# Projections two to six of the state-space layer as seven block products instead of eight

## The chip, the cores and the metric

The kernel runs on one core of one Trainium2 chip. The metric is the device time of one execution in microseconds. Three executions of the kernel before took 1654.04, 1657.95 and 1659.07 us, so the median is 1657.95 us. TensorE (PE in the rows, its weight loads PEld), VectorE (DVE), ScalarE (ACT), GpSimd (POOL) and SyncE (SP) each run their own list of instructions in order and wait for one another on semaphores.

## The reference, cut to what matters

Two blocks of two layers each are computed on 256 tokens of width 1024: gated convolutions, stick-breaking attention and two mixtures of experts, then a layer that joins a state-space scan with dilated attention, and a layer of block attention. The change touches only the opening of the state-space layer:

```python
def ssd_dilated_layer(x, norm_w, w_in, conv_w, conv_b, ...):
    h = rms_norm(x, norm_w)
    proj = jnp.einsum("bsd,df->bsf", h, w_in.astype(h.dtype))
    z, xbc, dt, q, k, v, g = split_cols(proj, EVEN_IN_SIZES)
    xbc = jax.nn.silu(causal_dwconv(xbc, conv_w, conv_b))       # 4 taps
    xs, bm, cm = split_cols(xbc, (SSD_D_INNER, ...))
    dt = jax.nn.softplus(dt + dt_bias)
    ...
    cb = jnp.einsum("bclgn,bcsgn->bgcls", Cc, Bc)
    ...
    y = y.reshape(Bsz, S, SSD_D_INNER) * jax.nn.silu(z)
```

All arithmetic is in float32. `xbc` has 2048 channels, `z` has 1024, so these two are 3072 of the columns of `w_in`.

## The kernel before, in words

The weights of a layer come in chunks of 2 MB (1024 x 512 numbers) that SyncE loads into a ring of slots. In the last two layers three slots hold chunks; the other three are free for sums of weights and of inputs. The state-space layer begins with six channel-wise chunks, g to g+5: the first four give `xbc`, the last two `z`. For each, TensorE holds 128 x 128 of the weights and streams all 256 tokens past them (`channels`, L712): 4 blocks of 128 channels x 8 steps over the 1024 inputs are 32 matmuls of 256 columns. Every float32 matmul leaves two records in the trace, so a chunk is 64 records of L719.

What follows a chunk, in the order written out by hand in `ssd_dilated` of each engine:

- ScalarE copies each of the four channel blocks from PSUM into `ss_pad` (L2001) and writes the last tap of the convolution with its bias into `xa` (L2004). After the fourth chunk it loads the table for silu and runs 16 silus (L2009); for chunks five and six it applies silu straight from PSUM into `ss_z` (L2012).
- VectorE adds the three other taps per block (L2814, L2817), each waiting for the one before. Between chunks two and three it computes dt (`steps`, L2795 to L2802).
- TensorE turns the `xs` part into token rows with transposes (`turn_x`, L1472) around chunk six; VectorE scales them into `ss_x` (L2833). Then come four pairs of matmuls B by C (L1492 and L1493), of which the third waits until all four parts of `ss_x` are done, since it writes the PSUM bank that they are read from. Then the scan begins: `run_sum` (L1505) on TensorE, `decay` (L2845, L2847) on VectorE.

Chunks g+6 to g+14 (queries, keys and values) already use seven block products in a layout with tokens on the output's partitions (`seven`, L1312): both operands are cut in halves, four sums of weight blocks (`w_sums`, L2645, one instruction of 128 x 1024 each) and four sums of input blocks (`x_sums`, L2620) are made on VectorE, and seven products of half size in each dimension replace eight. Three partial results are copied out of PSUM by ScalarE on the way (`keep`, L1862), because the next product adds to what stands there, and VectorE puts the blocks together. The weight sums of chunk g+6 are made before the last two parts of `ss_x`, those of g+7 before the first `decay`; there are ten buffers for them. During the scan, TensorE fills its time between `run_sum` and `y` with these products.

`keep_warm` (L736) issues matmuls that compute nothing, in the gap before this layer.

Of the kernel before, what the change touches and what calls it, by code (L numbers as in the profile page):

```python
# [20 lines left out]
P = 128  # L21
# [130 lines left out]
def build(nc, a, out, first=0, last=5):  # L152
# [6 lines left out]
    for n in on:  # L159
# [8 lines left out]
    sevens = [base[stage] + n for stage, which in ((SSD, range(6, 15)), (MOBA, (0, 1, 2, 4, 5, 6)))  # L168
              if stage in on for n in which]
    seven_no = {g: c for c, g in enumerate(sevens)}  # L170
# [19 lines left out]
    with ctx:  # L190
# [87 lines left out]
        def slot(g):  # L278
            return place_of[g]
# [138 lines left out]
        def seven_bank(g):  # L418

            if SSD in on and g < base[SSD] + 9:  # L420
                return 6
            return {0: 4, 1: 6, 2: 4}.get(g - base[MOBA], 0) if MOBA in on else 0

        def x_sums_no(g):

            return 13 if SSD in on and MOBA in on and g >= base[MOBA] else 0
# [10 lines left out]

        def seven_out(g):
# [8 lines left out]
            return whole[:, 0, 0:TOK], whole[:, 1, TOK:512], cross[:, :, 0:TOK], kind, grp  # L447

# [239 lines left out]
        def _(pe):  # L688
# [626 lines left out]

            spreads = [0]
# [112 lines left out]
            def ssd_dilated():  # L1429
# [10 lines left out]
                channels(g + 1, 6)  # L1440
# [8 lines left out]
                for c in (2, 3):  # L1449
                    pe.wait_ge(sem("ss_taken"), 8 * (c - 1))  # L1450
                    channels(g + c, 4 + 2 * (c % 2))
# [29 lines left out]
                pe.wait_ge(sem("ss_taken"), 8 * 4)  # L1481
                channels(g + 5, 6)
# [4 lines left out]
                pe.wait_ge(sem("ss_z"), 1)  # L1487
# [8 lines left out]
                pe.wait_ge(sem("ss_z"), 2)  # L1496
# [135 lines left out]
        def _(act):  # L1632
# [222 lines left out]
            def keep(g, n):  # L1855
# [4 lines left out]
                if n == 0 and proj_no(g) > 1:  # L1860
                    act.wait_ge(sem("at_proj"), proj_no(g) - 1)
                act.activation(kept[n], ps[:, b + (n == 1), 0:TOK], ACT.Copy)\  # L1862
# [113 lines left out]
            def ssd_dilated():  # L1976
# [15 lines left out]
                for c in range(4):  # L1992
                    if c == 2:
                        soft_dt()
                    done(g + c)
                    for m in range(4):
                        src = ps[:, 4 + 2 * (c % 2) + m // 2, (m % 2) * TOK:(m % 2 + 1) * TOK]
                        k = 4 * c + m
                        if c >= 2 and m == 0:
                            act.wait_ge(sem("ss_conv"), 4 * (c - 1))  # L2000
                        act.activation(ss_pad[:, c % 2, m, 3:3 + TOK], src, ACT.Copy)\  # L2001
                            .then_inc(sem("ss_taken"), 1)

                        act.activation(xa[:, k, :], src, ACT.Identity, bias=b[:, k:k + 1],  # L2004
                                       scale=w[:, k, 3:4]).then_inc(sem("ss_taken"), 1)
                silu_table()
                for m in range(16):
                    act.wait_ge(sem("ss_conv"), m + 1)
                    act.activation(xa[:, m, :], xa[:, m, :], ACT.Silu).then_inc(sem("ss_silu"), 1)  # L2009
                for c in range(2):  # L2010
                    done(g + 4 + c)
                    act.activation(ss_z[:, 4 * c:4 * c + 4, :]  # L2012
                                   .rearrange("p (b m) t -> p b (m t)", b=2), two_banks(4 + 2 * c),
                                   ACT.Silu).then_inc(sem("ss_z"), 1)
# [93 lines left out]
        def _(dve):  # L2108
# [493 lines left out]
            def x_sums(name):  # L2602
# [4 lines left out]
                n0 = 13 if name == "h5" and SSD in on else 0  # L2607
# [60 lines left out]
            def crossed(g):  # L2668
# [6 lines left out]
                    .then_inc(sem("at_proj"), 1)  # L2675

# [99 lines left out]
            def ssd_dilated():  # L2776
# [30 lines left out]
                for c in range(4):  # L2807
                    if c == 2:
                        steps()
                    for m in range(4):  # L2810
                        k = 4 * c + m
                        dve.wait_ge(sem("ss_taken"), 2 * k + 2)
                        for j in range(2):
# [6 lines left out]
                            .then_inc(sem("ss_conv"), 1)  # L2820
                dve.wait_ge(sem("ss_cs"), 1)
# [309 lines left out]
```

## Time and profile before

| what | value |
|---|---|
| median of three runs | 1657.95 us (1654.04 to 1659.07) |
| the profiled execution, its whole time | 1656.22 us |
| its span in the trace | 1654.4 us |
| mean granted TensorE clock | 0.996 of full speed |
| TensorE matmuls busy | 1562.2 us, 94% of the span |
| VectorE busy | 482.6 us, 29% |
| ScalarE busy | 266.7 us, 16% |

The span is the time from the first to the last instruction in the trace; 1.8 us of the execution lie outside it. A busy share says how much of the span an engine had an instruction in flight, not whether anything waited for it; who was waited for is told by the chain of waits and by the idle times before the instructions. The six channel-wise chunks lie between 1164 and 1254 us.

### The profile page before, as it was taken

Reading aid. Unit: us, or ns where it says so; the run is one execution under the profiler, and the core shown is the slowest. Engines: PE = TensorE matmul, PEld = TensorE weight load, DVE = VectorE, ACT = ScalarE, POOL = GpSimd, SP = SyncE. Lnnn points to the kernel's source line nnn. Section 1 sums busy time; section 2 is a strip of 40 time slices with the busy share of each in tenths; the row PEclk is TensorE's granted clock in tenths of the full one; section 3 lists DMA queues with packets and bytes.
Section 4 is the critical chain, followed back from the end, with each engine's and each line's share of the span. In section 5 each row is a group of like instructions: output and inputs, shape, how many; then the busy total and the mean of one; then the engine's idle time right before and its main releaser. Section 6 shows DMA issues by size and latency. Waiting matters only on the chain.

```text
span 1654.4 us, 25090 instructions
## 1 busy us (share of the span) xinstructions
PE 1562.2 (94%) x10686; PEld 1035.9 (63%) x10686; DVE 482.6 (29%) x932; ACT 266.7 (16%) x667; POOL 72.4 (4%) x138
## 2 busy tenths in 40 slices
PE   9999999998989999999999998898999999999998
PEld 8855555555555676465556555554888678748874
DVE  4941000000000313440000000002436887345642
ACT  1020000000000212210000000001232333221331
POOL 0000000000000000000000000000000431101120
PEclk9999999999999999999999999999999999999999
DMA  9689999999999942499999999999333224333420
GB/s 391 270 321 369 427 428 429 428 427 429 427 427 427 423 167 102 188 421 410 429 426 430 428 428 427 429 426 426 139 110 145 102 103 144 111 108 147 153 102 26
DMA packets 38517, 502.48 MB, mean 304 GB/s; under 512 B 4272, under 2 KB 4528, under 8 KB 6064
## 3 DMA queue, kind: packets, MB, share of 16 engines
q1 hardware_dynamic: 37872, 499.40, 73.3%
q0 software_dynamic: 576, 2.10, 0.3%
q8 instruction: 51, 0.84, 0.2%
q14 instruction: 18, 0.15, 0.0%
HBM read 500.43 MB, written 1.05 MB: 303 GB/s over the span
## 4 chain that ended last, share of the span: by engine, by line
PE 76%; DMA 12%; DVE 7%; issue 2%; ACT 2%; DVEq 0%; SPq 0%; ACTq 0%
PE ps L854 12%; PE ps L877 10%; PE ps L1312 10%; DMA ring<-in_expert_up 9%; PE ps L719 8%; PE ps L940 7%; PE ps L751 6%; PE ps L833 4%; PE ps L899 4%; DMA ring<-in_expert_down 3%; DVE arena L2253 2%; PE ps L1271 2%; PE ps L1099 2%; PE ps L1120 2%; PE ps L1393 1%
## 5 line engine op out<-in xcount | busy, mean ns | idle before, releaser
L854 PE MATMUL ps<-x_tok,tables_sb 128*128 128x256 f32 x1216 | 302.9, 392 | 0.0
L854 PEld LDWEIGHTS ps<-x_tok,tables_sb 128*128 128x128 f32 x1216 | 218.9, 190 | 104.1 <-issue 80.4
L877 PE MATMUL ps<-ring,arena 128*32 128x256 f32 x3968 | 238.6, 382 | 30.9 <-DMA ring<-in_expert_up 21.4
L877 PEld LDWEIGHTS ps<-ring,arena 128*32 128x32 f32 x3968 | 118.5, 109 | 139.9 <-issue 31.0
L719 PE MATMUL ps<-spare,ring 128*128 128x256 f32 x768 | 167.1, 380 | 0.9 <-DVE spare L2130 0.9
L2366 DVE TENSOR_TENSOR arena<-arena,ps 128x128 f32<-128x128 f32 x64 | 18.4, 287 | 497.8 <-ACT arena L1734 497.8
L719 PEld LDWEIGHTS ps<-spare,ring 128*128 128x128 f32 x768 | 145.5, 190 | 21.3 <-DVE spare L2130 1.2
L940 PE MATMUL ps<-ring,arena 128*32 128x512 f32 x928 | 116.4, 618 | 16.0 <-ACT arena L1729 11.4
L1312 PE MATMUL ps<-ring 128*128 128x256 f32 x480 | 110.5, 383 | 0.0
L1312 PEld LDWEIGHTS ps<-ring 128*128 128x128 f32 x480 | 89.5, 190 | 17.4 <-issue 5.5
L751 PE MATMUL ps<-ring,arena 128*128 128x512 f32 x224 | 98.6, 595 | 1.7 <-DVE arena L2303 1.2
L1734 ACT ACTIVATE arena<-ps 128x128 f32<-128x128 f32 x64 | 17.7, 277 | 457.6 <-PE ps L877 457.6
L1312 PE MATMUL ps<-ring,spare 128*128 128x256 f32 x360 | 83.6, 382 | 1.4 <-DVE tables_sb L2654 1.4
L1312 PEld LDWEIGHTS ps<-ring,spare 128*128 128x128 f32 x360 | 67.1, 190 | 12.9 <-issue 4.3
L751 PEld LDWEIGHTS ps<-ring,arena 128*128 128x128 f32 x224 | 41.8, 190 | 52.3 <-issue 49.1
L2645 DVE TENSOR_TENSOR ring<-ring 128x1024 f32<-128x1024 f32 x60 | 71.9, 1229 | 2.0 <-DMA ring<-in_stream 0.5
L899 PE MATMUL ps<-arena,root_w 128*128 128x512 f32 x128 | 59.8, 607 | 12.8 <-DVE arena L2375 11.4
L2375 DVE COPY arena<-ps 128x512 f32<-128x512 f32 x16 | 11.1, 692 | 204.2 <-PE ps L940 204.2
L940 PEld LDWEIGHTS ps<-ring,arena 128*32 128x32 f32 x928 | 26.0, 111 | 70.1 <-issue 68.7
L833 PE MATMUL ps<-arena,x_tok 128*128 128x128 f32 x512 | 60.6, 276 | 0.8 <-DVE arena L2325 0.8
L833 PEld LDWEIGHTS ps<-arena,x_tok 128*128 128x128 f32 x512 | 58.6, 192 | 1.9 <-DVE arena L2325 1.1
L899 PEld LDWEIGHTS ps<-arena,root_w 128*128 128x128 f32 x128 | 22.7, 189 | 51.2 <-DVE arena L2375 25.3
(299 smaller groups left out, 1397.3 us busy)
## 6 DMA issues: line engine op xcount, KB each, us to landing
ring<-in_expert_up SPq DMA_DIRECT2D x124, 2048.0 KB, 20.7
ring<-in_stream SPq DMA_DIRECT2D x43, 2048.0 KB, 8.3
ring<-in_expert_down SPq DMA_DIRECT2D x42, 2048.0 KB, 24.4
ring<-in_expert_down SPq DMA_DIRECT2D x32, 1024.0 KB, 22.7
arena<-in_expert_up SPq DMA_DIRECT2D x4, 2048.0 KB, 11.1
arena<-in_expert_down SPq DMA_DIRECT2D x2, 2048.0 KB, 12.4
tables_sb<-in_expert_down SPq DMA_DIRECT2D x2, 2048.0 KB, 9.9
spare<-in_expert_down SPq DMA_DIRECT2D x2, 2048.0 KB, 10.1
```

Of the source, the lines that this page charges most:

```text
L719: ins = pe.matmul(o, w[:, k, m * P:(m + 1) * P], xT[:, k, :], start=(k == 0), stop=(k == KT - 1))
L751: ins = pe.matmul(bank(2 * t + n), mixT[:, 4 * c + k, t * P:(t + 1) * P], w[:, k, n * 512:(n + 1) * 512], start=(c == 0 and k == 0), stop= ...
L833: ins = pe.matmul(ps[:, b, n * P:(n + 1) * P], x[:, t, k * P:(k + 1) * P], pick[:, t].rearrange("p e s -> p (e s)"), start=(t == 0), stop= ...
L854: pe.matmul(ps[:, b, 0:TOK], ident, x[:, 0, 0:TOK], start=True, stop=True, skip_group_check=True)
L877: ins = pe.matmul(ps[q * SLOTS:(q + 1) * SLOTS, 4 + e % 2, 0:TOK] .rearrange("p (g n) -> p g n", g=2), xg[:, 4 * half + k, e * SLOTS:(e + ...
L899: return pe.matmul(bank(2 * t + n), back[:, t * P:(t + 1) * P], yg[:, n * 512:(n + 1) * 512], start=False, stop=False, skip_group_check=True)
L940: ins = pe.matmul(ps[e * SLOTS:(e + 1) * SLOTS, 6 + n, :], hidT[:, e, k * SLOTS:(k + 1) * SLOTS], v, start=(k == 0), stop=(k == 3), skip_g ...
L1099: ins = pe.matmul(ps[:, 6 + q // 2, (q % 2) * TOK:(q % 2 + 1) * TOK], w[:, k, q * P:(q + 1) * P], xT[:, k, :], start=(k == 0), stop=(k == ...
L1120: ins = pe.matmul(bank(STICK_OUT[t] + n), sk_mixT[:, k, t * P:(t + 1) * P], w[:, k % 4, n * 512:(n + 1) * 512], start=(k == 0), stop=(k == ...
L1271: ins = pe.matmul(ps[:, b + part, (m % 2) * TOK:(m % 2 + 1) * TOK], w[:, k, m * P:(m + 1) * P], xT[:, k, :], start=(k == 0), stop=(k == KT ...
L1312: ins = pe.matmul(o, i[:, k, :], m[:, k, :], start=(opens and k == 0), stop=(k == 3), skip_group_check=True)
L2645: dve.tensor_tensor(w_sum[n % W_SUMS], a_, b_, sub).then_inc(sem("w_sums"), 1)
```

## The change

Chunks g+1 to g+5 are computed by seven block products as well, in the channel-wise layout: weight blocks are held in the array and 128 tokens stream past. Each product is 2 blocks of channels x 4 steps = 8 matmuls of 128 columns, so a chunk is 56 matmuls of 128 columns instead of 32 of 256. Before products 2, 3 and 5 TensorE waits for a copy by ScalarE (`kept`), before products 1, 2, 4 and 6 for a weight sum, and before product 6 for an addition by VectorE (`added`). The 20 weight sums of these five chunks, and five instructions per chunk that put its blocks together, are added to VectorE between its taps. ScalarE makes 15 copies (`keep`), and takes the last tap and the silu of `z` from SBUF instead of PSUM. The first chunk is as it was. The sums of the later chunks keep their places, with numbers raised by 20.

```diff
-    sevens = [base[stage] + n for stage, which in ((SSD, range(6, 15)), (MOBA, (0, 1, 2, 4, 5, 6)))
+    sevens = [base[stage] + n for stage, which in ((SSD, range(1, 15)), (MOBA, (0, 1, 2, 4, 5, 6)))
...
+            def seven_channels(g):
+                c, b, w = seven_no[g], seven_bank(g), slot8[slot(g)]
+                low, high, left, right = slice(0, 4), slice(4, 8), slice(0, TOK), slice(TOK, 512)
+                x1, x2 = xT[:, :, 0:P], xT[:, :, P:TOK]
+                t1, t2, t3, t4 = (w_sum[(4 * c + q) % W_SUMS] for q in range(4))
+                products = (
+                    (b, 0, w[:, low, left], x1[:, low], True),
+                    (b + 1, TOK, t1, x_sum[0], True),
+                    (b, 0, t2, x_sum[1], False),
+                    (b + 1, TOK, w[:, high, right], x_sum[2], False),
+                    (b + 1, 0, t3, x_sum[3], True),
+                    (b, TOK, w[:, high, left], x1[:, high], True),
+                    (b + 1, 0, t4, x2[:, high], False))
+                if c >= 2:
+                    pe.wait_ge(sem("ss_proj"), c - 1)
+                arrive(pe, g)
+                for n, (o_b, at, w_, x_, opens) in enumerate(products):
+                    if 0 < n < 5:
+                        pe.wait_ge(sem("added"), n)
+                    if n in (2, 3, 5):
+                        pe.wait_ge(sem("kept"), 3 * c + (2, 3, 5).index(n) + 1)
+                    if n in (1, 2, 4, 6):
+                        pe.wait_ge(sem("w_sums"), 4 * c + (1, 2, 4, 6).index(n) + 1)
+                    if n == 6:
+                        pe.wait_ge(sem("added"), added_no(g))
+                    for m in range(2):
+                        for k in range(4):
+                            ins = pe.matmul(ps[:, o_b, at + m * P:at + (m + 1) * P],
+                                            w_[:, k, m * P:(m + 1) * P], x_[:, k, :],
+                                            start=(opens and m == 0 and k == 0), stop=(k == 3),
+                                            skip_group_check=True)
+                    ins.then_inc(chunk_done if n == 6 else sem("product"), 1)
...
-                channels(g + 1, 6)
+                seven_channels(g + 1)
...
-                pe.wait_ge(sem("ss_taken"), 8 * 3)
-                channels(g + 4, 4)
+                seven_channels(g + 4)
```

ScalarE's order behind the first chunk:

```diff
+                keep(g + 1, 1)
+                keep(g + 1, 2)
+                last_taps(1)
+                for n in range(3):
+                    keep(g + 2, n)
+                last_taps(2)
+                keep(g + 3, 0)
+                soft_dt()
+                keep(g + 3, 1)
+                keep(g + 3, 2)
+                last_taps(3)
                 silu_table()
...
+                keep(g + 4, 0)
+                silus(range(4))
+                keep(g + 4, 1)
+                silus(range(4, 8))
+                keep(g + 4, 2)
+                silus(range(8, 16))
+                gate_silu(0)
+                for n in range(3):
+                    keep(g + 5, n)
+                gate_silu(1)
```

VectorE's new helpers, and its order:

```diff
+            def channel_corner(g):
+                c, b, o = seven_no[g], seven_bank(g), channel_rows(g)
+                dve.wait_ge(sem("product"), 6 * c + 5)
+                dve.wait_ge(sem("kept"), 3 * c + 2)
+                dve.tensor_tensor(kept[1], kept[1], ps[:, b + 1, 0:TOK], add)\
+                    .then_inc(sem("added"), 1)
+                dve.wait_ge(sem("added"), added_no(g))
+                dve.wait_ge(sem("kept"), 3 * c + 3)
+                dve.tensor_tensor(o[:, 2:4, P:], kept[1].rearrange(halves_of, m=2),
+                                  kept[2].rearrange(halves_of, m=2), add)
...
+            def channel_crossed(g):
+                c, b, o = seven_no[g], seven_bank(g), channel_rows(g)
+                dve.wait_ge(chunk_done, g + 1)
+                dve.tensor_tensor(o[:, 0:2, P:], kept[2].rearrange(halves_of, m=2),
+                                  ps[:, b + 1, 0:TOK].rearrange(halves_of, m=2), add)
+                dve.tensor_tensor(o[:, 2:4, 0:P], kept[2].rearrange(halves_of, m=2),
+                                  ps[:, b + 1, TOK:].rearrange(halves_of, m=2), add)\
+                    .then_inc(sem("ss_proj"), 1)
...
+                w_sums(8)
+                taps_of(0)
+                channel_corner(g + 1)
+                channel_front(g + 1)
+                channel_crossed(g + 1)
+                w_sums(12)
+                taps_of(1)
...
+                channel_corner(g + 3)
+                channel_front(g + 3)
+                w_sums(14)
+                channel_crossed(g + 3)
+                w_sums(16)
+                taps_of(3)
...
                 for u in range(4):
-                    if u == 2:
-                        w_sums(4)
+                    if u % 2 == 0:
+                        channel_corner(g + 4 + u // 2)
+                        channel_front(g + 4 + u // 2)
+                        channel_crossed(g + 4 + u // 2)
+                        w_sums(20 + 2 * u)
```

VectorE before, from the last step of the convolution to the first `decay` (L2822 and L2825 ready the decays, L2833 writes `ss_x`, L2645 is a weight sum, L2845 the first `decay`):

```order
L2822 TENSOR_SCALAR tables_sb<-ps 128x32 [waits ss_cs]
L2825 COPY arena<-ps 16x256 [waits dve_step]
L2833 TENSOR_TENSOR arena<-ps,tables_sb 128x512 [waits ss_turned] x2
L2645 TENSOR_TENSOR ring<-ring 128x1024 [waits w_in5]
L2645 TENSOR_TENSOR ring<-ring 128x1024 [waits w_sums]
L2645 TENSOR_TENSOR ring<-ring 128x1024
L2645 TENSOR_TENSOR ring<-ring 128x1024 [waits w_sums]
L2833 TENSOR_TENSOR arena<-ps,tables_sb 128x512 [waits ss_turned] x2
L2645 TENSOR_TENSOR ring<-ring 128x1024 [waits w_in0]
```

VectorE now, the end of the same place, from the assembly of chunk g+5 on (L2764 and L2768 are the corner, L2775 the front, L2782 and L2784 the crossed blocks, L2724 a weight sum, L2966 writes `ss_x`):

```order
L2764 TENSOR_TENSOR tables_sb<-tables_sb,ps 128x256 [waits kept,product]
L2768 TENSOR_TENSOR arena<-tables_sb 128x2x128 [waits kept,added]
L2775 TENSOR_TENSOR arena<-tables_sb,ps 128x2x128 [waits product]
L2782 TENSOR_TENSOR arena<-tables_sb,ps 128x2x128 [waits chunk_done]
L2784 TENSOR_TENSOR arena<-tables_sb,ps 128x2x128
L2724 TENSOR_TENSOR ring<-ring 128x1024 [waits product,w_in5]
L2724 TENSOR_TENSOR ring<-ring 128x1024 [waits w_sums,chunk_done]
L2724 TENSOR_TENSOR ring<-ring 128x1024 [waits product]
L2724 TENSOR_TENSOR ring<-ring 128x1024 [waits w_sums,product]
L2966 TENSOR_TENSOR arena<-ps,tables_sb 128x512 [waits ss_turned] x2
L2724 TENSOR_TENSOR ring<-ring 128x1024 [waits product,w_in0]
```

The four sums ahead of the last two parts of `ss_x` now stand behind two instructions that wait for the end of chunk g+5.

ScalarE now, where chunks g+3 and g+4 meet (L1910 is `keep`, L2046 the last taps, L2054 silu, L1687 names the load of silu's table):

```order
L1910 ACTIVATE tables_sb<-ps 128x256 [waits product] x2
L2046 ACTIVATE arena<-arena,tables_sb 128x256 [waits ss_proj]
L2046 ACTIVATE arena<-arena,tables_sb 128x256 x3
L1687 ACT_TABLE_LOAD
L1910 ACTIVATE tables_sb<-ps 128x256 [waits ss_proj,product]
L2054 ACTIVATE arena<-arena 128x256 [waits ss_conv] x4
```

The first copy of chunk g+4 stands behind four last taps, which wait for the assembly of chunk g+3, and behind the table load; before, nothing on TensorE waited for that load.

## Rows read from the trace of the kernel before

**Rows 1.** The page: busy time by engine, and the chain that ended last by engine.

```profile
PE 1562.2 (94%) x10686; PEld 1035.9 (63%) x10686; DVE 482.6 (29%) x932; ACT 266.7 (16%) x667; POOL 72.4 (4%) x138
...
PE 76%; DMA 12%; DVE 7%; issue 2%; ACT 2%; DVEq 0%; SPq 0%; ACTq 0%
```

**Rows 2.** The chain of waits from 1150 us on: start, us, what.

```profile
1164.22 27.89 PE ps L719 x128
1192.11 3.48 PE ps L1446 x32
1195.59 27.72 PE ps L719 x128
...
1253.35 0.87 PE ps L1472 x8
...
1255.54 0.43 PE ps L1492 x2
...
1256.85 0.63 PE ps L1505 x4
1257.47 7.10 PE ps L1312 x32
```

**Rows 3.** Timeline of TensorE, expert stage: start, us, instruction, columns, records.

```profile
1072.33 3.74 PE L833 MATMUL ps<-arena,x_tok 128*128 128x128 f32 x32
1075.90 0.27 PE L895 MATMUL ps<-tables_sb,arena 128*128 128x128 f32 x1
```

**Rows 4.** The 16-column matmuls of L1446: records, ns min/median/max, first and last start.

```profile
L1446 PEld LDWEIGHTS ps<-tables_sb,spare x32: 190/192/192, 1191.7 to 1195.3; 128*128 128x128 f32 x32
```

**Rows 5.** Timeline of TensorE, block attention's first projections by seven products.

```profile
1494.72 7.17 PE L1312 MATMUL ps<-ring 128*128 128x256 f32 x32
...
1529.59 13.98 PE L1271 MATMUL ps<-spare,ring 128*128 128x256 f32 x64
```

**Rows 6.** Timeline of all engines around the last channel-wise chunks.

```profile
1209.82 0.56 ACT L2004 ACTIVATE arena<-ps,tables_sb 128x256 f32<-128x256 f32 x1
1210.26 0.38 ACT L2001 ACTIVATE arena<-ps 128x256 f32<-128x256 f32 x1
1210.41 1.00 DVE L2814 SCALAR_TENSOR_TENSOR arena<-arena,tables_sb 128x256 f32<-128x256 f32 x2 [10.04 <-ACT arena L2004]
...
1215.76 0.48 DVE L2817 SCALAR_TENSOR_TENSOR arena<-arena,tables_sb 128x256 f32<-128x256 f32 x1
...
1226.39 1.28 ACT L1642 ACT_TABLE_LOAD   x1
...
1240.34 4.74 DVE L2645 TENSOR_TENSOR ring<-ring 128x1024 f32<-128x1024 f32 x4
...
1253.83 1.29 DVE L2833 TENSOR_TENSOR arena<-ps,tables_sb 128x512 f32<-128x512 f32 x2 [8.74 <-PE ps L1472]
...
1259.69 0.48 DVE L2845 SCALAR_TENSOR_TENSOR arena<-ps,tables_sb 128x256 f32<-128x256 f32 x1
...
1267.17 0.42 DVE L2654 TENSOR_TENSOR tables_sb<-tables_sb,ps 128x256 f32<-128x256 f32 x1 [0.54 <-PE ps L1312]
```

**Rows 7.** TensorE by stretches: length, busy (records), granted clock, DMA share, GB/s.

```profile
532.00:534.00 2.00, 0.52 (x3) 1.00 1.02 434
534.00:536.00 2.00, 1.26 (x12) 0.86 0.96 410
536.00:538.00 2.00, 2.00 (x12) 0.50 1.04 442
...
544.00:546.00 2.00, 2.00 (x11) 0.58 1.01 422
...
1136.00:1138.00 2.00, 1.73 (x11) 0.54 0.99 418
1138.00:1140.00 2.00, 2.00 (x13) 0.60 0.95 401
...
1155.00:1160.00 5.00, 2.75 (x13) 1.00 1.03 434
```

More of the change, by code:

```diff
@@ L424, in x_sums_no @@
         def x_sums_no(g):
[L426 removed]
+            return 18 if SSD in on and MOBA in on and g >= base[MOBA] else 0
         def added_no(g):
@@ L1448, in ssd_dilated @@
                 ins.then_inc(sem("ss_dt"), 1)
-                for c in (2, 3):
-                    pe.wait_ge(sem("ss_taken"), 8 * (c - 1))
-                    channels(g + c, 4 + 2 * (c % 2))
+                pe.wait_ge(sem("ss_taken"), 8)
+                seven_channels(g + 2)
+                seven_channels(g + 3)
                 pe.wait_ge(sem("ss_a"), 2)
@@ L2002, in ssd_dilated, with silus @@
                             .then_inc(sem("ss_taken"), 1)
-                        act.activation(xa[:, k, :], src, ACT.Identity, bias=b[:, k:k + 1],
-                                       scale=w[:, k, 3:4]).then_inc(sem("ss_taken"), 1)
-                silu_table()
[L2007 to L2014, printed above, removed]
+                def silus(which):
+                    for m in which:
+                        act.wait_ge(sem("ss_conv"), m + 1)
+                        act.activation(xa[:, m, :], xa[:, m, :], ACT.Silu)\
+                            .then_inc(sem("ss_silu"), 1)
@@ new lines, in gate_silu @@
+                def gate_silu(c):
+                    act.wait_ge(sem("ss_proj"), 4 + c)
+                    z = ss_z[:, 4 * c:4 * c + 4, :]
+                    act.activation(z, z, ACT.Silu).then_inc(sem("ss_z"), 1)
+                done(g)
+                for m in range(4):
+                    src = ps[:, 4 + m // 2, (m % 2) * TOK:(m % 2 + 1) * TOK]
+                    if m == 3:
+                        keep(g + 1, 0)
+                    act.activation(ss_pad[:, 0, m, 3:3 + TOK], src, ACT.Copy)\
+                        .then_inc(sem("ss_taken"), 1)
+                    act.activation(xa[:, m, :], src, ACT.Identity, bias=b[:, m:m + 1],
+                                   scale=w[:, m, 3:4]).then_inc(sem("ss_taken"), 1)
@@ L2806, in ssd_dilated, with taps_of @@
                 w = C("conv2_w")
-                for c in range(4):
-                    if c == 2:
-                        steps()
+                def taps_of(c):
                     for m in range(4):
                         k = 4 * c + m
-                        dve.wait_ge(sem("ss_taken"), 2 * k + 2)
+                        dve.wait_ge(sem("ss_taken"), k + 5 if c else 2 * m + 2)
                         for j in range(2):
```

55 lines of the change are left out of this document (36 added, 19 removed).

## The prediction

> **What bounds the kernel now.** I read the page first: TensorE is busy for 94% of the span, and it is 76% of the chain that ended last [rows 1]. Then the chain of waits around the layer that the change touches: from 1164.22 us to the first `run_sum` at 1256.85 us it lies on TensorE almost without a gap, and the scan that follows begins with its matmuls too [rows 2]. So here a microsecond of matmuls saved is worth a microsecond, and any wait that TensorE meets costs its full length. VectorE and ScalarE have slack in this stretch: VectorE sat idle for 10.04 us before the taps at 1210.41 us [rows 6].
>
> **What the products save.** Two chunks before are 128 records in 27.89 us, 0.218 us a record [rows 2], so one chunk of 64 records is 13.95 us. Now it is 56 matmuls of 128 columns, 112 records. The only long strip of such matmuls with full weights is that of L833: from 1072.33 us to the next instruction at 1075.90 us, 32 records in 3.57 us, 0.1116 us each [rows 3]. 112 x 0.1116 = 12.50 us, so a chunk saves 1.45 us and five save 7.2 us. This is a twelfth less than the eighth that the arithmetic drops, since a record of half the columns takes 0.51 of the time and not 0.5.
>
> That strip has one wait in it; the new chunks have seven each, 35 in all, and what a satisfied wait costs between matmuls so short isn't in the trace. From below it is zero: in the block attention's projections 160 records of 256 columns stand between 1494.72 and 1529.59 us [rows 5], 34.87 us or 0.218 us each, the same as without waits, though 20 products begin in them. From above it is a whole weight load that isn't hidden, 0.19 us [rows 4], or 6.6 us for all 35. It can't be less than nothing, since a wait brings no work forward. I take zero, by the row that has the same waits, and keep the other end for the range.
>
> **What the waits on the way cost.** Within a chunk, a copy by ScalarE takes 0.38 us and an addition of 256 columns on VectorE 0.42 us [rows 6], against 16 x 0.1116 = 1.8 us of the product that runs beside them, so they are hidden if their engine is free. The ten buffers for weight sums are enough, and every chunk is loaded three chunks ahead. Per chunk VectorE has four sums, 4.74 us, twelve tap instructions, 1210.41 to 1216.24 us or 5.8 us [rows 6], and five assembly instructions, about 2 us: 12.6 us against TensorE's 12.5. The first chunks have cover: TensorE also has the first chunk and the 3.5 us of L1446 [rows 2]. I followed the three queues with these durations and found three places to look at.
>
> Chunk g+3, product 6: the addition before it stands behind the taps of chunk two, and these behind `steps`, which waits for ScalarE. By the sum it comes 0.1 us too late or just in time. I count nothing, but there is no margin.
>
> Chunk g+4, product 2: it needs the copy of product 0. Ahead of that copy ScalarE has four last taps and the table load. VectorE makes two weight sums before it assembles the crossed blocks of g+3, so the taps can begin only some 2.2 us after that chunk's last product; four of them at the 0.45 us from L2004's start to the next copy's start make 1.8 us, the table 1.28 us, the copy with its handover 0.5 us [rows 6]: 5.8 us. TensorE has 0.9 us for the cumulative sums and two products of 1.8 us to do, 4.5 us. It waits 1.3 us.
>
> Before the third pair of B by C: this pair needs all of `ss_x`. Before, its last two parts came as soon as the transposes were done: from the end of the sixth chunk, at 1253.35 us, to the third pair at 1255.54 us it was 2.2 us [rows 2]. Now VectorE first has to assemble the crossed blocks of g+5, which waits for the end of that chunk, 0.8 us, then makes four weight sums, 4.74 us, and then two parts of `ss_x`, 1.29 us [rows 6]; with 0.3 us of handovers, 7.1 us. The same four sums stood in the same place before, but at 1240.34 us they ran under the matmuls of the sixth chunk [rows 6]. This stall of 4.9 us is the largest cost of the change, and it comes at the very place where the chain runs from TensorE over VectorE and back.
>
> The sum on TensorE: -7.2 + 1.3 + 4.9 = -1.0 us at the first `run_sum`. On VectorE the first `decay` comes 11.9 us after the end of chunk g+5 (0.8 + 4.74 + 1.29 + 4.74 + 0.3), which now ends at 1253.35 - 7.2 + 1.3 = 1247.4 us, so at 1259.3 us against 1259.69 us [rows 6]. The scan behind it is unchanged and can keep at most what TensorE gained.
>
> **What an idle TensorE costs afterwards.** Twice in the trace the granted clock halves, from 2.4 to 1.2 GHz, after TensorE was little used: it was busy for 0.52 and 1.26 us of the two stretches before 536 us, and then ran at half until about 545 us; and it was at half for about 3.5 us from 1136 us on [rows 7]. Against it: at 1155 us, with 2.25 us of idle in 5 us, the clock stayed at full [rows 7]. The new stall of 4.9 us is longer than any idle time in the whole trace, so I expect the clock to fall. From 3.5 to 10 us at half speed, half of that is lost: 1.7 to 5 us. I take 2.5 us, nearer to the short one, since dense matmuls follow.
>
> The Trainium skill (TensorE: Matmul & The Clock Gate, section "What's actually happening") says the same: the slow clock is the default state, an idle engine falls back to it, and activity brings the fast one back. The two places in the trace agree with it, the one at 1155 us sets a limit to it.
>
> **The sum.** -1.0 + 2.5 = +1.5 us. From the profiled execution's 1656.22 us this gives 1657.7 us; the median of the runs shown is 1.73 us above that execution, so the time to compare with it is 1659.5 us. A change of under 0.3%, 5 us, can't be told from none by a measurement of this kernel.
>
> **The rivals.**
>
> One, the clock holds: the stall is a stall and no more. For it speaks the stretch at 1155 us, against it that the idle time is more than twice as long here. The sum is then -1.0 us, 1657 us.
>
> Two, the stall isn't there: if the 4.9 us are hidden because the wait for `ss_x` is met by something earlier, what stays is -7.2 + 1.3 = -5.9 us, 1652 us, faster. For it speaks only that the same sums cost nothing before; against it, the order of VectorE's instructions, in which the sums stand between the end of the chunk and `ss_x`.
>
> Three, slower: every product begins with a weight load that isn't drawn ahead past its wait. Columns of 256 cover such a load and columns of 128 don't, and then the rows of the block attention say nothing about the new chunks. The place is the 35 product starts, the price up to 0.19 us each [rows 4], 6.6 us. With the stall and the clock the time is 1659.5 + 6.6 = 1666 us. It decides from 0.1 us a start on: 35 x 0.1 = 3.5 us and +1.5 us make +5 us. For it speaks that a weight load of 0.19 us is longer than the 0.1116 us between records, so that loads must already overlap; against it, that nothing of the kind is seen where 256 columns are used.
>
> Four, the weight loads set the pace of all short matmuls. The Trainium skill (TensorE: Matmul & The Clock Gate, section "Back-to-back issue gap") has sustained spacing set by both the load and the matmul, with 81 ns at 128 columns where the isolated matmul takes about 56 ns; by that ratio of 1.45 on half of 0.218 us, a record would take 0.158 us, a chunk 17.7 us, and the kernel would be some 19 us slower. As a mechanism of this kernel it has its bound in rows: the loads of the 16-column matmuls follow one another from 1191.7 to 1195.3 us, 31 steps in 3.6 us or 0.116 us each [rows 4]. At that pace a chunk is 13.0 us and the five save 4.7 us instead of 7.2; the kernel comes to 1662 us. The strip of L833 at 0.1116 us speaks against both.
>
> **How the numbers follow.** The forecast 50%; the clock holds 22%; the stall isn't there 8%; slow product starts 13%; weight loads set the pace 7%. Faster by over 0.3% (below 1653.0 us) is the second rival and a little from durations that all fall on the good side: 10%. Slower by over 0.3% (above 1662.9 us) is the third, half of the fourth, and part of the forecast with the long slow clock: 19%. Within 0.3% is the rest, 71%. The range of 8 in 10 runs from 1653.5 us, just short of the second rival, to 1666 us, the third.
>
> **What would show it.** In the profile after: the matmuls of L1357 (`seven_channels`) in unbroken strips at 0.1116 us a record, or with a gap of 0.1 us and more every 16 records (rival three) or a higher pace throughout (rival four). TensorE idle for about 4.9 us before the third B by C matmul (L1537), put down to VectorE, with four weight sums (L2724) in that time; no such gap is rival two. A granted clock of half speed right behind it for 3 to 10 us; 1.00 there is rival one. An idle time of about 1.3 us in chunk g+4, put down to ScalarE's copy. VectorE's first `decay` near 1259 us. If instead the projections themselves took over 13 us each, or other gaps of over 1 us stood between 1178 and 1247 us, the working above is wrong.

## The result, and the profile after

The changed kernel took 1659.53 us, the median of 20 runs (1656.20 to 1665.76), beside 1656.95 us for the kernel before on the same chip (20 runs, 1653.18 to 1661.13). The ratio is 1.002, with a 95% interval of 1.0011 to 1.0029: a little slower, by 3.3 us at that ratio and by 2.6 us between the two medians. The prediction was 1659.5 us in a range of 1653.5 to 1666. It had held that under 0.3% can't be told from none here; with 20 runs on each side 0.2% could. The changed kernel's profiled execution took 1664.13 us, 4.6 us over the median of its kind, so its excess over the profile of before can't be read as the change's cost without sorting it.

The page of the changed kernel, answering to [rows 1]: the span, busy time by engine, and the chain by engine.

```profile
span 1662.3 us, 25671 instructions
...
PE 1561.6 (94%) x10926; PEld 1045.1 (63%) x10926; DVE 515.3 (31%) x977; ACT 269.0 (16%) x670; POOL 71.9 (4%) x138
...
PE 74%; DMA 14%; DVE 8%; issue 2%; ACT 2%; SPq 0%; DVEq 0%; ACTq 0%
```

TensorE is as busy as before although it has less to do. That is already a sign of a slower clock: in the stretches further down, 2 us hold 18 records where the clock is at 0.9, and 10 or 11 where it is at half. The chain of waits, answering to [rows 2] (start, us, what; L731 is `channels`, L1357 `seven_channels`, L1493 the dt matmuls, L1537 and L1538 B by C, L1550 `run_sum`, L1324 `seven`):

```profile
1166.11 14.08 PE ps L731 x64
1180.19 12.50 PE ps L1357 x112
1192.69 3.92 PE ps L1493 x32
1196.61 27.92 PE ps L1357 x224
...
1225.88 3.77 PE ps L1357 x32
1229.64 0.59 issue
1230.24 9.17 PE ps L1357 x80
...
1240.28 12.52 PE ps L1357 x112
...
1258.32 1.21 DVE arena L2966 x2
1259.57 1.22 PE ps L1537 x2
...
1262.50 1.16 PE ps L1550 x4
```

Three things differ from a plain list of shorter chunks. Chunks g+2 and g+3 took 27.92 us together where two at 12.50 us would be 25.0. There is a wait of 0.59 us in chunk g+4. And between the end of chunk g+5 and the third pair of B by C the chain leaves TensorE. TensorE by stretches of 2 us shows what happened in the first of them (length, busy time with records, granted clock, DMA share, GB/s), as [rows 7] did elsewhere:

```profile
1194.00:1196.00 2.00, 2.00 (x18) 0.89 0.60 229
1196.00:1198.00 2.00, 2.00 (x10) 0.50 0.99 418
1198.00:1200.00 2.00, 2.00 (x11) 0.50 0.68 279
...
1202.00:1204.00 2.00, 2.00 (x18) 0.90 0.00 0
```

The granted clock was at half, 1.2 GHz, for some 6.8 us. It fell under the last of the dt matmuls, without any idle time of TensorE ahead of it; below this is called the half clock behind dt. In the profile of before it stayed at full there. The timeline of all engines around the wait shows the second place (start, us, instruction; in brackets the idle time before it and what ended it; L2782 is the first crossed block, L2724 a weight sum, L2966 writes `ss_x`, L2978 is the first `decay`), answering to the last lines of [rows 6]:

```profile
1252.83 0.42 DVE L2782 TENSOR_TENSOR arena<-tables_sb,ps 128x256 f32<-128x256 f32 x1 [1.37 <-PE ps L1357]
...
1253.49 4.82 DVE L2724 TENSOR_TENSOR ring<-ring 128x1024 f32<-128x1024 f32 x4
...
1254.59 0.39 PE L1538 MATMUL ps<-arena 128*128 128x128 f32 x2
...
1258.23 1.28 DVE L2966 TENSOR_TENSOR arena<-ps,tables_sb 128x512 f32<-128x512 f32 x2
...
1259.57 1.22 PE L1537 MATMUL ps<-arena 128*128 128x256 f32 x2 [4.60 <-DVE arena L2966]
...
1264.16 0.48 DVE L2978 SCALAR_TENSOR_TENSOR arena<-ps,tables_sb 128x256 f32<-128x256 f32 x1
```

The order of VectorE is there to be read: crossed blocks, four sums of 4.82 us, `ss_x`, and only then the matmuls, which had stood ready since 1254.9 us. The same matmuls that took 0.60 us just before now take 1.22. TensorE by stretches of 3 us behind it:

```profile
1255.00:1258.00 3.00, 0.00 (x0) 0.83 0.93 393
1258.00:1261.00 3.00, 1.43 (x4) 0.50 0.46 197
1261.00:1264.00 3.00, 3.00 (x11) 0.50 0.04 8
...
1267.00:1270.00 3.00, 3.00 (x14) 0.96 0.00 0
```

To sort the executions I measured each profile from the first channel-wise matmul of the layer to the first pair of B by C, to the first `run_sum`, and to the gate's matmuls in block attention, all from the timeline. In us:

| kernel | to the first pair | to the first `run_sum` | to the gate |
|---|---|---|---|
| before | 89.9 | 92.6 | 365.4 |
| before_again | 89.8 | 92.5 | 365.3 |
| before_halves | 89.8 | 92.6 | 365.4 |
| changed | 87.4 | 96.3 | 371.4 |
| again | 87.4 | 95.7 | 371.1 |
| warm | 87.4 | 95.0 | 367.8 |
| after_halves | 84.1 | 92.7 | 367.7 |
| sums_behind | 85.7 | 88.8 | 366.9 |
| spread | 87.2 | 90.3 | 366.1 |
| early | 85.5 | 88.6 | 361.7 |
| halves | 83.9 | 87.0 | 360.1 |
| stall_in_before | 93.2 | 101.1 | 375.8 |

Two profiles of one kernel agree here to 0.3 us at the gate, while their whole times differ by more. The rest of a profile explains that: behind the gate's first matmul all twelve take the same 124.8 us, and the layer begins at 1162.6 to 1169.8 us. In the four profiles with the old products it begins at 1163.9 to 1164.6 us, in four of the eight with the new ones at 1167 us or later. Whether that is chance is open; the table leaves it out, the ratios of whole times hold it. To the gate the changed kernel's profile is 6.0 us longer than that of before. This is a sum of three: the planned work and its waits, the clock behind the wait, and the clock behind the dt matmuls. The experiments take them apart.

### The profile page after: what moved, and what is told of

It is laid out like the page before. It is cut to its first block, busy times and chain, and to the rows that moved or that the text cites. A ratio compares the mean times of both kernels' runs of the same rounds, so it can differ in the third digit from the quotient of the medians.

```text
span 1662.3 us, 25671 instructions
## 1 busy us (share of the span) xinstructions
PE 1561.6 (94%) x10926; PEld 1045.1 (63%) x10926; DVE 515.3 (31%) x977; ACT 269.0 (16%) x670; POOL 71.9 (4%) x138
## 4 chain that ended last, share of the span: by engine, by line
PE 74%; DMA 14%; DVE 8%; issue 2%; ACT 2%; SPq 0%; DVEq 0%; ACTq 0%
PE ps L866 12%; DMA ring<-in_expert_up 10%; PE ps L889 10%; PE ps L1324 10%; PE ps L952 7%; PE ps L763 6%; PE ps L1357 4%; PE ps L845 4%; PE ps L731 3%; DMA ring<-in_expert_down 3%; PE ps L911 3%; DVE arena L2332 2%; PE ps L1283 2%; PE ps L1111 2%; PE ps L1132 2%
## 5 line engine op out<-in xcount | busy, mean ns | idle before, releaser
L1324 PE MATMUL ps<-ring 128*128 128x256 f32 x480 | 110.6, 384 | 0.0
L1324 PEld LDWEIGHTS ps<-ring 128*128 128x128 f32 x480 | 90.0, 191 | 17.3 <-issue 5.5
L731 PE MATMUL ps<-spare,ring 128*128 128x256 f32 x448 | 99.1, 384 | 1.1 <-DVE spare L2209 1.1
L2724 DVE TENSOR_TENSOR ring<-ring 128x1024 f32<-128x1024 f32 x80 | 95.5, 1227 | 2.2 <-DVE ring L2724 0.5
L731 PEld LDWEIGHTS ps<-spare,ring 128*128 128x128 f32 x448 | 86.4, 193 | 13.4 <-DVE spare L2209 1.3
L1324 PE MATMUL ps<-ring,spare 128*128 128x256 f32 x360 | 85.4, 388 | 1.5 <-DVE tables_sb L2733 1.5
L1324 PEld LDWEIGHTS ps<-ring,spare 128*128 128x128 f32 x360 | 68.4, 194 | 13.5 <-issue 4.7
```

Of the source, the lines that this page charges most:

```text
L731: ins = pe.matmul(o, w[:, k, m * P:(m + 1) * P], xT[:, k, :], start=(k == 0), stop=(k == KT - 1))
L1324: ins = pe.matmul(o, i[:, k, :], m[:, k, :], start=(opens and k == 0), stop=(k == 3), skip_group_check=True)
L2724: dve.tensor_tensor(w_sum[n % W_SUMS], a_, b_, sub).then_inc(sem("w_sums"), 1)
```

## The experiments

The theory: the saving in the products is real and is given back by the wait for `ss_x` and the half clock behind it. Its first rival is that the clock there costs nothing of its own. Its second is that the wait is not the cost, since it would only come back elsewhere. Each ratio is to the kernel before, timed on the same chip, with its 95% interval.

**again**: the changed kernel, unaltered.

> The changed kernel once more, unaltered, for a second profile beside the next ones. Theory A: the wait for ss_x (4.6 us) and the half clock right behind it (about 10 us, so 5 us lost) belong to the order of the instructions and come again in the same place. The half clock of 6.6 us behind the 16-column matmuls of dt, at 1195.6 us of the first profile, is open: the kernel before has the same matmuls and kept its full clock there. If it hangs on the order it comes again, if it is chance it may be missing here, and then this profile is some 3.3 us shorter than the first, whose span was 1662.3 us. Rival: both falls of the clock are chance; then the one behind the wait may be missing too.

Median 1660.86 us of 12 (1655.78 to 1665.59), ratio 1.0024 [1.0011, 1.0036]. In its profile stand the same 4.6 us of wait, and both half clocks. TensorE by stretches, beside the dt matmuls and around the wait:

```profile
1198.00:1200.00 2.00, 2.00 (x11) 0.50 0.98 418
```

```profile
1250.00:1260.00 10.00, 5.97 (x50) 1.00 0.53 195
1260.00:1270.00 10.00, 9.43 (x31) 0.66 0.04 17
```

So the result repeats, and the half clock behind dt wasn't an accident of one execution. The half clock at the wait is shorter here: the clock held through the idle time and fell some 0.7 us after TensorE had resumed at 1260.57 us, for 6.8 us, where in the first profile it fell 2.6 us before the resume, for 10.2 us.

**warm**: eleven matmuls that compute nothing of use stand where TensorE waits, everything else as in the changed kernel.

```diff
                     if q == 2:
+                        for _ in range(11):
+                            pe.matmul(ps[:, 0, 0:TOK], ident, con[:, 0:TOK], start=True,
+                                      stop=True, skip_group_check=True)
                         pe.wait_ge(sem("ss_x"), 4)
```

> The changed kernel with 11 matmuls of 256 columns that compute nothing, into an unused bank, between the second and the third pair of B by C, 4.8 us at 0.437 us each; they fill the wait for ss_x and shorten nothing. Theory A (wait and clock are two costs): the third pair starts as late as before, the clock stays at full, and the time falls by the 5 us that the half clock took, to about 0.999 of the kernel before. Rival (the half clock costs nothing, since VectorE sets the pace of the scan's beginning): the clock stays at full and the time is that of the changed kernel, 1.002 of the one before.

Median 1658.11 us of 12 (1652.6 to 1664.2), ratio 1.0001 [0.999, 1.0012]. Its timeline and its clock by stretches behind (L1536 the idle matmuls, L1540 the third pair, its numbers shifted by the insertion):

```profile
1258.51 4.91 PE L1536 MATMUL ps<-tables_sb 128*128 128x256 f32 x22
1263.27 0.70 PE L1540 MATMUL ps<-arena 128*128 128x256 f32 x2
```

```profile
1263.00:1266.00 3.00, 3.00 (x17) 1.00 0.09 36
```

The third pair comes as late as before, but at full clock, and the gate is reached 3.3 to 3.6 us sooner than in **again** and in the changed kernel: 367.8 against 371.1 and 371.4. This is the price of the clock alone, with the wait kept. It agrees with half of the time in which TensorE was busy at low clock: in the changed kernel 7.5 of some 10 us, from 1259.57 to 1267 us, which makes 3.8 us, and in **again** all of 6.8 us, which makes 3.4. The 5 us that were expected counted the idle part too.

**sums_behind**: the four sums of chunk g+6 move behind the last two parts of `ss_x`.

```diff
-                        w_sums(20 + 2 * u)
+                    if u == 0:
+                        w_sums(20)
```

> The changed kernel with the four weight sums of chunk g+6 moved behind the last two parts of ss_x, nothing else. Theory A: the third pair starts 2.3 us after the chunk's end instead of 6.9, the wait of 4.6 us and the half clock (5 us) go; all eight sums now stand ahead of the first decay, which comes as late as before (11.8 us after the chunk's end), so TensorE, with 7.1 us of products to do behind the first two run_sums, waits there for about 2 us. Sum: -4.6 - 5 + 2 = -7.6 us against the changed kernel, 1652 us, 0.997 of the kernel before. Rival (the beginning of the scan is bound by VectorE, so the wait has only moved): only the clock's part is won or not even that, -5 to 0 us, 0.999 to 1.002.

Median 1657.68 us of 12 (1656.42 to 1664.71), ratio 1.0014 [1.0002, 1.0026]. The wait for `ss_x` is gone, and the first `run_sum` comes 7.5 us earlier than in the changed kernel. At the gate only 4.5 are left, and 1.7 of these lie ahead of the first pair, where the move does nothing: the half clock behind dt lasted only 3.4 us in this execution. So the move itself gained 2.8 us, and the ratio stands 0.0006 below that of the changed kernel and 0.0010 below **again**'s, 1.0 and 1.7 us, with intervals that overlap. A part of the half clock behind dt, then TensorE's longest wait by line, and ScalarE's timeline:

```profile
1194.00:1198.00 4.00, 4.00 (x27) 0.69 0.54 225
```

```profile
PE ps L1324 <- ACT tables_sb L1910: 3.5, 1, 3.5
```

```profile
1254.78 0.39 ACT L1910 ACTIVATE tables_sb<-ps 128x256 f32<-128x256 f32 x1 [1.94 <-PE ps L1324]
1260.16 1.17 ACT L2113 ACTIVATE arena<-arena 128x384 f32<-128x384 f32 x2 [4.99 <-DVE arena L2981]
1261.23 0.64 ACT L1910 ACTIVATE tables_sb<-ps 128x256 f32<-128x256 f32 x2
```

VectorE now makes eight sums in a row ahead of the first `decay`. ScalarE's exponentials (L2113) wait for that decay, the second copy of chunk g+6 stands behind them, and TensorE waits 3.5 us for the copy, with a half clock behind that too (0.54 from 1262 to 1265 us). The rival was nearer than the theory: the wait had moved.

**spread**: as sums_behind, and the four sums of chunk g+7 that stood before the first `decay` go between the scan's steps, so that two stand in a step; the first copy of chunk g+4 goes before the table load.

```diff
-                silu_table()
                 keep(g + 4, 0)
+                silu_table()
...
-                w_sums(28)
+                w_sums(24)
...
-                        w_sums(20 + SCAN_SUMS[n])
+                        w_sums((26, 28, 30, 32, 34, 35)[n])
```

> As the kernel before this one in the list (sums behind ss_x), and besides the four sums of chunk g+7 move from before the first decay into the scan, where each step now makes two sums (26, 28, 30, 32, 34, 35 as the counts reached), and ScalarE makes the first copy of chunk g+4 before it loads silu's table. Theory A: no wait at ss_x, none at the first decays, none of 0.6 us in chunk g+4: -4.6 - 5 - 0.6 = -10.2 us against the changed kernel, 1649 us, 0.995 of the kernel before, which is the 7.2 us of matmuls saved. Rival (VectorE is the bound in the scan, where it is busy for 34 of 43 us): the sums put in between the decays hold up the scan, by up to 4.7 us, and the gain is that of the other one or less, 0.997.

Median 1656.04 us of 12 (1651.46 to 1660.93), ratio 0.9994 [0.9981, 1.0008]. TensorE's longest wait by line:

```profile
PE ps L1550 <- DVE arena L2981: 2.2, 2, 1.2
```

The wait in chunk g+4 fell from 0.59 to 0.3 us. But with two sums in a late step of the scan, `run_sum` waits for a `decay` twice, for 1.0 and 1.2 us within 7 us, and behind the second wait the clock was at half for 3.4 us:

```profile
1310.00:1320.00 10.00, 8.80 (x45) 0.84 0.14 27
```

So the ratio stayed above the 0.995 that was expected.

**early**: as spread, with the counts `(27, 30, 32, 34, 35, 35)`, so three sums in each of the first two steps, then two, and one or none in the last.

> As the kernel with sums spread into the scan, but with the counts 27, 30, 32, 34, 35, 35 instead of 26, 28, 30, 32, 34, 35: one sum more in each of the first two steps and none late, since the two waits of TensorE for decays in that kernel, 1.0 and 1.2 us, came in the last two steps, behind sums. Theory A: both waits go, the scan takes 49 us instead of 50.8 from the first to the last run_sum, -2 us against that kernel: 0.998 of the kernel before. Rival: the early sums hold up the early decays instead and nothing is won.

Median 1652.6 us of 11 (1649.83 to 1655.35), ratio 0.9974 [0.9963, 0.9986]. Both late waits and the half clock behind them are gone, and from the first `run_sum` to the gate it is 273.1 us against 272.8 in the kernel before: the scan is undisturbed. The half clock behind dt lasted 3.4 us here too, so to the first pair it is 85.5 us. VectorE goes from the crossed blocks straight to `ss_x` (here L2967):

```profile
1248.86 0.41 DVE L2784 TENSOR_TENSOR arena<-tables_sb,ps 128x256 f32<-128x256 f32 x1
...
1249.19 1.28 DVE L2967 TENSOR_TENSOR arena<-ps,tables_sb 128x512 f32<-128x512 f32 x2
```

**stall_in_before**: the kernel before, with its own products of 256 columns. Only VectorE is made to wait for the end of chunk g+5 before its four sums.

```diff
                     if u == 2:
+                        dve.wait_ge(chunk_done, g + 6)
                         w_sums(4)
```

> The kernel before, in which VectorE also waits for the end of chunk g+5 before it makes the four weight sums that stand ahead of the last two parts of ss_x: the order that the change brought, without the new products. Theory A (the wait for ss_x costs its full length and then a half clock of about 10 us): the third pair of B by C starts 6.3 us instead of 2.2 us after the chunk's end, and 1.7 to 5 us are lost behind it: 1.0035 to 1.0055 of the kernel before. Rival (TensorE's fills in the scan absorb the wait): under 1.0015.

Median 1661.86 us of 8 (1659.63 to 1667.22), ratio 1.0035 [1.0019, 1.005]. TensorE's longest wait by line, and its clock by stretches behind it:

```profile
PE ps L1492 <- DVE arena L2834: 3.9, 1, 3.9
```

```profile
1265.00:1268.00 3.00, 3.00 (x10) 0.50 0.00 0
```

Without any of the new products, the order of VectorE alone costs 5.8 us at the ratio. To the gate its profile is 10.4 us longer than that of before: 3.9 us for the wait, 3.3 for a half clock behind dt, which this profile had as well (its price is measured below), and the 3.2 that are left for the half clock behind the wait, which lasted 6.8 us. The half clock behind dt thus doesn't need products of 128 columns.

**before_again**: the kernel before, unaltered.

> The kernel before, unaltered, for a second profile. Question: does its clock also fall to half behind the 16-column matmuls of dt (L1446, 3.5 us)? Theory C (the fall needs products of 128 columns ahead of them): full clock there again, as in the first profile. Rival (it is chance in either kernel): half clock for about 6 us in some profiles of either.

Median 1658.71 us of 10 (1653.59 to 1663.29), ratio 1.0011 [0.9997, 1.0024], an interval that holds 1; so ratios that differ by 0.1% are not told apart by runs of this size. Full clock behind the dt matmuls, as in the first profile.

**halves**: as early, and the dt matmuls of the second 128 tokens stand behind chunk g+2 instead of behind g+1.

```diff
-                for t in range(2):
+                def dt(t):
...
+                dt(0)
                 pe.wait_ge(sem("ss_taken"), 8)
                 seven_channels(g + 2)
+                dt(1).then_inc(sem("ss_dt"), 1)
```

> As the kernel before this one in the list, with the 16 matmuls of 16 columns for dt split into two groups of 8, 1.75 us each, one behind chunk g+1 as now and one behind chunk g+2. Theory C (3.5 us of such matmuls in one piece make the clock fall for 6.6 us): the clock stays at full between 1190 and 1215 us, -3.3 us in every run in which it fell: 0.996 to 0.998 of the kernel before. Rival (the fall there is chance or comes from the products of 128 columns): the half clock is there again, at the same place or beside it, and the time is that of the other kernel.

Median 1649.44 us of 8 (1649.05 to 1655.26), ratio 0.9961 [0.9949, 0.9974]. The chain of waits and the clock by stretches (here L1493 is still dt, 16 records each time):

```profile
1176.71 12.51 PE ps L1357 x112
1189.21 1.69 PE ps L1493 x16
1190.90 12.60 PE ps L1357 x112
1203.50 1.69 PE ps L1493 x16
```

```profile
1196.00:1200.00 4.00, 4.00 (x39) 1.00 0.02 8
```

There is no half clock from 1184 to 1216 us. This version beats both kernels: 7.4 us below before in the medians, 6.5 by the ratio, 5.3 us less to the gate. Its interval overlaps that of **early**; to the gate it is 1.6 us ahead of it, and to the first pair too, which is half of early's 3.4 us at half clock.

**before_halves** and **after_halves**: the same division of dt, in the kernel before (where the second half stands between chunks g+2 and g+3) and in the changed kernel, with nothing else altered.

> The kernel before with the 16 matmuls of dt in two groups of 8, behind chunks g+1 and g+2, nothing else. Of three profiles with the kernel's old products one shows the half clock behind dt (the one with the added wait), two don't. Theory D (the fall belongs to the 3.5 us of 16-column matmuls in one piece, in either kernel, but doesn't come in every run): no half clock in the profile between 1185 and 1215 us, and on average about a third of 3.4 us less: 0.9990 to 1.0000 of the kernel before. Rival (the fall has nothing to do with dt): 1.000, and a half clock there in some profile.

> The changed kernel with dt in two groups, nothing else. All five profiles with the new products and dt in one piece show a half clock behind dt, of 3 to 7 us. Theory D: it is gone, 1.7 to 3.4 us less than the changed kernel in most runs: 0.9995 to 1.0010 of the kernel before, where the changed kernel has 1.002. Rival (products of 128 columns let the clock fall by themselves): the half clock is still there and the ratio stays at 1.002. The half clock behind the wait for ss_x stays in either case.

before_halves: 1656.21 us of 12 (1652.32 to 1661.46), beside 1658.42 us for before; 0.9993 [0.998, 1.0007]. after_halves: 1659.49 us of 12 (1653.03 to 1663.13), 1.0006 [0.9993, 1.0018], where the changed kernel has 1.002 and 1.0024. For the kernel before no gain can be told from none, and for the changed kernel the intervals overlap: the gain is seen in the profiles, not surely in the times. In after_halves's profile the clock is full behind both halves, the wait is still there, and the half clock behind the wait too:

```profile
1196.00:1200.00 4.00, 4.00 (x37) 1.00 0.77 319
...
1258.00:1261.00 3.00, 2.65 (x10) 0.62 0.11 41
1261.00:1264.00 3.00, 3.00 (x9) 0.50 0.00 0
```

```profile
PE ps L1541 <- DVE arena L2970: 4.6, 1, 4.6
```

To the first pair it needs 84.1 us against 87.4 in the changed kernel: the half clock behind dt costs 3.3 us in an execution in which it lasts 6.8 us, and 1.7 us where it lasts 3.4.

## Why the prediction was right, step by step

**The sum closes.** The work and waits alone were predicted at -1.0 us. Term by term, at full clock, they measured -6.2 for the products, +0.6 in chunk g+4 and +4.6 for `ss_x` (all below), also -1.0. In **warm** the clock behind the wait is full, the one behind dt is not: 367.8 - 365.4 - 3.3 = -0.9 us. **after_halves**, behind its first pair, is a check that went into neither number: work and waits, and 3.4 us for its 6.8 us at half clock behind the wait, make +2.4 to +2.5 us, and it measured 367.7 - 365.4 = +2.3. Together in the changed kernel: -0.9 + 3.3 for the clock behind dt + 3.3 to 3.6 for the one behind the wait = +5.7 to +6.0 us against the 6.0 of its profile and the 5.7 of **again**. The ratio's +3.3 us lies between this and the +2.3 to 2.4 us of an execution without the clock fall behind dt.

**The products' saving**, predicted at 7.2 us: right in pace, a little too large in sum. Strips without another operation between them, in the timeline of the changed kernel:

```profile
1181.81 7.31 PE L1357 MATMUL ps<-ring 128*128 128x128 f32 x64
1188.96 3.74 PE L1357 MATMUL ps<-spare,ring 128*128 128x128 f32 x32
```

From 1181.81 to 1188.96 us are 64 records, 0.1117 us each, with four product starts and their satisfied waits among them: the rival of costly product starts fell, since a start costs nothing, and so did that of the weight loads' pace. A chunk measured 12.50 us as predicted. But the five together, added up in the chain of **after_halves** (12.51 + 12.60 + 12.60 + 3.77 + 9.17 + 12.52), are 63.2 us, and the five in the chain of before 69.4: 6.2 us saved. Of the 1.0 us that is missing, 0.7 went at the new chunks' edges, where another kind of matmul or a wait stands before: 12.60 instead of 12.50 behind dt, 12.94 in chunk g+4. The rest is that the old five took less than five times 13.95 us. And where the prediction calls a chunk's saving a twelfth less than the dropped eighth, its own 1.45 of 13.95 us is a sixth less; its sum doesn't use that phrase.

**Chunk g+3** was predicted at nothing with no margin: no wait stands there, at full clock either (12.60 us in **after_halves**). **Chunk g+4** was predicted to wait 1.3 us and waited 0.59. The timeline of all engines shows the steps (L2046 the last taps, L1687 the table load, L1910 the copy):

```profile
1226.37 2.08 ACT L2046 ACTIVATE arena<-arena,tables_sb 128x256 f32<-128x256 f32 x4 [8.56 <-DVE arena L2784]
...
1228.46 1.28 ACT L1687 ACT_TABLE_LOAD   x1
...
1229.76 0.38 ACT L1910 ACTIVATE tables_sb<-ps 128x256 f32<-128x256 f32 x1
...
1230.24 5.60 PE L1357 MATMUL ps<-ring 128*128 128x128 f32 x48 [0.59 <-issue]
```

The releaser isn't named (issue), but the copy's end at 1230.14 us is what came last. The queue was as worked out; the taps started 1.8 us after the last product's end (1196.61 + 27.92 = 1224.53 us in the chain), not 2.2, and TensorE's short matmuls until 1225.88 us took 1.35 us, not 0.9.

**The wait for `ss_x`**, predicted at 4.9 us, is 4.60 us, with the four sums in it. That it costs what it lasts is shown twice, by taking it away (sums_behind, early) and by putting it into the kernel before. The rival that it isn't there fell.

**The clock**, predicted at 2.5 us from 1.7 to 5: this term was too small by 0.8 to 1.1 us. It measured 3.3 to 3.6 us (warm), and the rival of a clock that holds fell. I had weighed the short half clock of 3.5 us in [rows 7] more than the long one of nearly 10. The lengths measured behind this wait were 10.2, 6.8 and again 6.8 us (changed, again, after_halves), and only the busy part costs. The idle time that brought it was 4.6 us; 3.9 us did so too in stall_in_before, 3.5 in sums_behind, there for 3.4 us only.

**Not in the prediction** was the half clock behind the dt matmuls. It is in all six profiles that have the new products and dt undivided (changed, again, warm and spread for 6.8 us, sums_behind and early for 3.4), in one of three with the old products and dt undivided, and in none of the three with dt divided. So dividing dt takes it away, as far as three profiles show. Why the new products should invite it more than the old is open: in both the 3.5 us of 16-column matmuls are the same, and three profiles of the old are few. If it is rarer in the kernel before, it is a true part of the change's cost, and could account for the 1 us by which the ratio exceeds the +2.4 us of work, waits and the clock behind the wait; so could a later start of the layer. No run here decides it.

**The first `decay`** was a sign named near 1259 us, 95.1 us behind the layer's start. It came at 1264.16 us, 98.1 us behind a start at 1166.11: mostly the 3.3 us of the half clock behind dt.

The median hit 1659.5 us more closely than the working deserves, and that is luck in two ways. Between the terms, the saving was 1.0 us smaller, the two waits 1.0 us shorter, the clock 1 us dearer. And the forecast was +1.5 us on a base of 1657.95 us, the median of three executions; the median of twenty is 1656.95, and the change cost 2.6 us between the medians, 3.3 at the ratio. A base 1.0 us too high made up for a change that was forecast 1.1 us too small.

## What to carry to other kernels

When an engine with slack is given more work, look at the order in its queue and not at its busy share: the same four sums were free at 1240 us, under matmuls, and cost 4.6 us behind a wait for the end of the chunk, which with the half clock behind it is more than the whole saving of 6.2 us. When a wait is removed, follow who stood behind it; here it came back as 3.5 us, and then as 2.2 us, before the sums were spread so that the saving was kept. After an idle time of TensorE like the 3.9 and 4.6 us here, add half of the busy time that follows at low clock, 3.2 to 3.6 us here, and look at more than one profile, since the same place had low clocks of different lengths. When two profiles are compared over a stretch, see first whether other half clocks lie in it: 1.7 of the 4.5 us that sums_behind seemed to gain did not come from its edit.

## What the runs showed of the hardware

- Float32 matmuls of 128 columns with full weights run at 0.1117 us a record against 0.218 us at 256 columns, and a wait on a semaphore that is already satisfied adds nothing, though each weight load by itself takes 0.19 us.
- The granted clock fell to half under 3.5 us of 16-column matmuls or right behind them, with TensorE never idle, and stayed there for 6.8 us (changed, again, warm, spread, stall_in_before) or 3.4 us (sums_behind, early); in before and before_again it did not fall. With the same 32 records in two groups of 1.69 us, 12.6 to 13.9 us apart, it did not fall in three profiles.
- Waits of 3.5, 3.9 and 4.6 us of TensorE in this layer brought the half clock in each of the five profiles in which TensorE was idle in them. In the changed kernel it fell 2.6 us before TensorE resumed, in sums_behind 0.4 us before, in again, after_halves and stall_in_before 0.3 to 0.7 us after. Full speed was back 7.1 to 7.7 us after TensorE had resumed behind the 3.9 and 4.6 us, and some 3 us after it behind the 3.5 us. In warm, with TensorE kept busy in the same 4.6 us, it did not fall.
- Two waits of 1.0 and 1.2 us within 7 us, in spread, were followed by 3.4 us at half clock.
